# The sums of squares of three norms, moved from GpSimd's queue into VectorE's

## What is computed

```python
def rmsnorm(x, g):
    return x * lax.rsqrt(jnp.mean(x * x, axis=-1, keepdims=True) + EPS) * g

# layer 0: x += concat(short gated convolution, windowed attention)(rmsnorm(x)) @ w_out
# layer 1: x += pool_mix(rmsnorm(x)): window means of 2, 4, 8, 16 tokens minus x, a map per group, a scale
# after each: x += square(relu(rmsnorm(x) @ w_up)) @ w_down      (1024 -> 4096 -> 1024)
```

## Time and profile before

| | us |
|---|---|
| median of three executions | 1857.74 (1857.17 to 1860.59) |
| the profiled execution | 1856.85 |
| its span | 1855.1 |
| TensorE busy (matmul) | 1794.6 |
| VectorE busy | 1286.3 |
| ScalarE busy | 698.8 |
| GpSimd busy | 97.2 |
| the mean granted clock of TensorE | 0.988 of full speed |

### The profile page before, as it was taken

The page is one execution under the profiler, slowest core; times in us unless marked ns, Lnnn a source line. Parts: engine busy times, 40 slices in busy tenths (PEclk is TensorE's granted clock), DMA queues, the critical chain, the costliest instruction groups (busy, mean ns, idle before and its releaser), DMA issues.

```text
span 1855.1 us, 33339 instructions
## 1 busy us (share of the span) xinstructions
PE 1794.6 (97%) x13805; PEld 1752.4 (94%) x13805; DVE 1286.3 (69%) x1992; ACT 698.8 (38%) x1169; POOL 97.2 (5%) x127
## 2 busy tenths in 40 slices
PE   6999999997999999999999999799999999999999
PEld 5998888997999999999999999699999999999999
DVE  4447775469766666878586766787667677868684
ACT  5433332135333333524243355443333353424331
POOL 1100000140000000000000122100000000000000
PEclk9999999999999999999999999799999999999999
DMA  5311111320443444744445212034434484534432
GB/s 196 107 39 35 35 35 53 97 82 25 166 150 135 154 147 153 272 155 162 149 155 179 80 42 79 20 122 152 167 140 143 156 279 144 186 116 169 158 113 95
DMA packets 154519, 233.75 MB, mean 126 GB/s; under 512 B 6800, under 2 KB 103360, under 8 KB 150624
## 3 DMA queue, kind: packets, MB, share of 16 engines
q1 hardware_dynamic: 150880, 222.31, 34.7%
q0 software_dynamic: 3200, 9.21, 1.7%
q10 hardware_dynamic: 288, 0.09, 0.0%
HBM read 160.40 MB, written 71.47 MB: 125 GB/s over the span
## 4 chain that ended last, share of the span: by engine, by line
PE 79%; DVE 11%; ACT 3%; DMA 3%; issue 2%; SPq 1%; POOL 0%; POOLq 0%; DVEq 0%; ACTq 0%
PE out L783 16%; PE out L785 16%; PE out L784 16%; PE scores L785 4%; PE turned L785 4%; PE scores L784 4%; PE turned L784 4%; PE scores L783 4%; PE turned L783 4%; DVE b_lo L2050 1%; DVE ring L2035 1%; DMA wide<-in_w_down 1%; PE turned L965 1%; DVE b_full L2002 1%; DMA wide<-in_w_up 1%
## 5 line engine op out<-in xcount | busy, mean ns | idle before, releaser
L783 PE MATMUL out<-b_hi,ring 128*128 128x268 f32 (+1 forms) x2048 | 590.2, 288 | 23.5 <-DVE b_lo L2066 7.1
L785 PE MATMUL out<-b_hi,ring 128*128 128x268 f32 (+1 forms) x2048 | 589.7, 288 | 0.0
L784 PE MATMUL out<-b_lo,ring 128*128 128x268 f32 (+1 forms) x2048 | 589.3, 288 | 0.0
L1401 ACT ACTIVATE ring<-wide 128x512 fp32r<-128x512 f32 x384 | 233.1, 627 | 552.3 <-DVE wide L2024 225.9
L783 PEld LDWEIGHTS out<-b_hi,ring 128*128 128x128 f32 x2048 | 390.5, 191 | 26.6 <-DVE ring L2035 13.3
L784 PEld LDWEIGHTS out<-b_lo,ring 128*128 128x128 f32 x2048 | 390.1, 190 | 0.1
L785 PEld LDWEIGHTS out<-b_hi,ring 128*128 128x128 f32 x2048 | 390.2, 191 | 0.0
L2035 DVE TENSOR_TENSOR ring<-wide,ring 128x512 fp32r<-128x512 f32 x384 | 261.8, 690 | 154.2 <-ACT ring L1401 152.9
L783 PE MATMUL out<-act_hi,w_hi 128*128 128x352 f32 (+2 forms) x656 | 219.4, 334 | 10.5 <-DVE act_lo L1750 9.2
L783 PE MATMUL turned<-b_hi,ring 128*128 128x268 f32 (+1 forms) x768 | 219.3, 286 | 3.2 <-ACT rs L1385 3.2
L783 PE MATMUL scores<-b_hi,ring 128*128 128x268 f32 (+1 forms) x768 | 219.1, 285 | 2.0 <-DVE ring L2035 2.0
(11 more groups left out here) (204 smaller groups left out, 2593.9 us busy)
## 6 DMA issues: line engine op xcount, KB each, us to landing
wide<-in_w_up SPq DMA_DIRECT2D x32, 1024.0 KB, 5.8
wide<-in_w_down SPq DMA_DIRECT2D x32, 1024.0 KB, 5.6
b_full<-h_dram SPq DMA_DIRECT2D x28, 1072.0 KB, 5.1
b_full<-h_dram SPq DMA_DIRECT2D x28, 1056.0 KB, 5.4
h_dram<-hid SPq DMA_DIRECT2D x64, 268.0 KB, 2.1
h_dram<-hid SPq DMA_DIRECT2D x64, 264.0 KB, 2.2
h_dram<-hid SPq DMA_DIRECT2D x16, 804.0 KB, 3.7
h_dram<-hid SPq DMA_DIRECT2D x16, 792.0 KB, 3.5
```

Of the source, the lines that this page charges most:

```text
L783: nc.tensor.matmul(out, lhs[0], rhs[0], start=first, stop=False, skip_group_check=skip)
L784: nc.tensor.matmul(out, lhs[0], rhs[1], start=False, stop=False, skip_group_check=skip)
L785: return nc.tensor.matmul(out, lhs[1], rhs[0], start=False, stop=last, skip_group_check=skip)
L1401: nc.scalar.activation(cells(ring, n, 0), left_source(U, q), ACT.Copy).then_inc(left_hi, 1)
```

## The change

GpSimd's adds are taken out, with all their waits; nothing but DMA stands in its queue. VectorE gets the same 66 adds, each as its own instruction on the same columns, with the same waits. ScalarE's and TensorE's queues are the same as before, in order and in their waits. Line numbers of the changed kernel are lower by up to 28 ahead of the new functions, and higher by up to 12 behind them.

```diff
-            def add_square(k, c0, c1, begin):
-                pool.wait_ge(sum_begun, begin + 1)
-                pool.wait_ge(squared, k + 1)
-                if k:
-                    pool.wait_ge(added, added_at(k) - 1)
-                n = 1 if k < 28 else 2 if k < 42 else 3
-                nc.gpsimd.tensor_tensor(rs[:, c0:c1], rs[:, c0:c1], square_view(n, k, c1 - c0), ALU.add).then_inc(added, 1)
...
+            def add_square(k, n, p):
+                c0, c1 = NORM_PIECES[n][p] if n != 2 else (HALF_COLS * p, HALF_COLS * (p + 1))
+                dve.wait_ge(sum_begun, begun_no(n, p) + 1)
+                dve.wait_ge(squared, k + 1)
+                if k:
+                    dve.wait_ge(added, added_at(k) - 1)
+                nc.vector.tensor_tensor(rs[:, c0:c1], rs[:, c0:c1], square_view(n, k, c1 - c0), ALU.add).then_inc(added, 1)
...
+                    if a == UNITS - 4 and t in (5, 11, 12, 13):
+                        add_pair_square(a, {5: 1, 11: 3, 12: 4, 13: 5}[t])
+                    if a == UNITS - 2 and t == 1:
+                        add_pair_square(a - 2, 6)
+                        add_pair_square(a - 2, 7)
+                    if a == UNITS - 2 and t in (4, 5, 10, 11, 12, 13):
+                        add_pair_square(a, {4: 0, 5: 1, 10: 2, 11: 3, 12: 4, 13: 5}[t])
...
                     add_output(p, oc)
+                    if p and oc == 0:
+                        add_squares(1, p - 1, 6, 7)
+                    if oc >= 2 and (p < 3 or oc < 7):
+                        add_squares(1, p, oc - 2, oc - 1)
...
+            add_pair_square(UNITS - 2, 6)
+            add_pair_square(UNITS - 2, 7)
             for i in range(10):
...
+                if i == 7:
+                    add_squares(3, 1, 3, 7)
                 add_windows(i)
+                if i in (3, 6, 8):
+                    add_squares(3, {3: 0, 6: 1, 8: 2}[i], 0, 3)
+                if i == 4:
+                    add_squares(3, 0, 3, 7)
...
                 if i == 6:
                     normed(3, 0, 1)
+                if i == 7:
                     left_lo_part(UNITS, A12)
                     first_right_lo(B11, UNITS, 0)
-                if i == 7:
                     first_right_lo(B21, UNITS, 0)
...
+            add_squares(3, 2, 3, 7)
             first_right_lo(B21, UNITS, 1)
+            add_squares(3, 3, 0, 5)
             first_pair(UNITS)
```

More of the change, by code:

```diff
@@ L1980, in _, with add_squares, add_pair_square @@
                         split_lo(W_OUT + 4 + oc // 2)
+            def add_square(k, n, p):
[5 more added lines that the diff above has]
+                nc.vector.tensor_tensor(rs[:, c0:c1], rs[:, c0:c1], square_view(n, k, c1 - c0), ALU.add).then_inc(added, 1)
+            def add_squares(n, p, first, end):
+                for i in range(first, end):
+                    add_square(add_no(n, p) + i, n, p)
+            def add_pair_square(a, t):
+                l, k = pair_square_no(a, t)
+                if k is not None:
+                    add_square(k, 2, l)
             def add_output(p, oc):
```

## The result

The changed kernel took **1878.21 us** (median of 4 runs, 1877.06 to 1882.65). The kernel before took 1858.7 us (median of 4 runs, 1857.17 to 1860.59; one run more than ahead of the prediction). The ratio is 1.0107, with a 95% interval of 1.0094 to 1.0119: slower by 19.9 us, where 17.6 were forecast (1875.3 us). The profiled execution took 1879.21 us; its span of 1877.4 us is 22.3 us longer than that of before.

What follows compares the result with a forecast made beforehand. TensorE (97% busy) was taken to bound the kernel, VectorE from 1142 to 1167 us. Waits 10.8 plus clock 6.8 gave 17.6 us; 1856.85 became 1874.5, with 0.9 for the median 1875.3; range 1872 to 1878.5 (8 in 10: 1865 to 1881).

Steps and rivals of the forecast that it cites:

- More is lost: Rival, 12%: row sums' dip (+1.7), first norm's +1.5, and adds in a row waiting for squares; 1878 to 1882 us.
- this ring: Pooling: VectorE's late add holds ScalarE's square, then the z scaling, then TensorE; +2.9, +3.1, +1.7, +4.0 us at four places.
- Map 5 and map 6: Pooling: TensorE starts these maps late, waiting for z scalings behind squares that need VectorE's adds; +2.9 and +3.1 us.
- Row sums: End of first MLP: the last add TensorE needs stands behind VectorE's last product addition; +1.6 us.
- The size of an add: Price of one add on VectorE by width: 0.44 us at 268 columns, 0.47 at 312, 0.37 at 216.
- First norm: Norm ahead of the first MLP: 26 adds cost 0, bounds -1 to +1.5 us.
- Tail: From tile 9's additions to ScalarE's eight scalings: 5.3 us instead of 7.8, so -2.5 us.
- 4 x 1.7 = 6.8 us: Clock: each of four new TensorE stalls followed by a low clock losing 1.7 us; 6.8 us, bounds 0 to 8.5.
- Waits: New waits at row sums and pooling, less the tail's gain: 1.6 + 2.9 + 3.1 + 1.7 + 4.0 - 2.5 = 10.8 us.
- engine time alone: Rival, 5%: ScalarE is let go in time; only VectorE's added work, row sums and tail count; +3.1 us, 1860.8.
- The waits come, the clock stays: Rival, 25%: the new waits cost 10.8 us but no low clock follows the stalls; 1868.5 us.

Runs made afterwards that it cites:

- Experiments 4 and 6: Against the changed kernel: 4 put second-MLP-norm adds ahead of VectorE's window additions, 1864.31 us; 6 moved ScalarE's scalings of maps 4, 5 ahead of blocked squares, 1870.16 us.
- n1_only: Kernel before with only the 26 adds of the first MLP's norm moved to VectorE, the other 40 left on GpSimd; 1856.03 us (one run).
- warm2: Changed kernel plus 27 unread TensorE matmuls in the four stalls, the last nine ahead of the wait for the windows' input; 1871.5 us, ratio 1.0055.
- tail_only: Kernel before with only the last nine adds of the second MLP's norm moved to VectorE; 1858.9 us, ratio 0.9994.
- early: Changed kernel with the second MLP's norm adds placed earlier in VectorE's queue, ahead of the window additions; 1864.31 us, ratio 1.0023.
- early_warm: early_rowsum plus eight unread TensorE matmuls: six ahead of the mean product behind map 8, two ahead of tile 9's windows; 1861.73 us, ratio 1.0003.
- before_warm: Kernel before plus eight unread TensorE matmuls: six ahead of the mean product behind map 8, two ahead of tile 9's windows; 1861.18 us, ratio 1.0003.
- n2_only: Kernel before with only the 14 adds of the pooling's norm moved to VectorE, all others left on GpSimd; 1864.64 us (one run).
- act_order: Changed kernel with, on ScalarE alone, the scalings of maps 4 and 5 moved ahead of the blocked squares; 1870.16 us (one run).
- warm: Changed kernel plus 27 unread TensorE matmuls for the four stalls, the last nine behind the wait for z; 1876.3 us, ratio 1.009.
- n3_only: Only the second MLP's norm's 26 adds on VectorE, steps placed as in the changed kernel, other norms on GpSimd; 1879.35 us, ratio 1.0098.
- early_rowsum: early with the last pooling-norm add that the row sums wait for one product addition earlier on VectorE; 1861.17 us, ratio 1.0006.

## Why the prediction was right, and where it was off

The direction, the place and the kind of the loss were forecast. The time came out 2.9 us above the forecast of 1875.3 and 0.3 us inside its range, and part of that is luck: the profiled spans grew by 22.3 us where 17.6 were forecast, while the median lies 1.0 us below the profiled execution where 0.9 above was assumed. The measured 1878.21 also lies in the range of the second rival, "More is lost" (1878 to 1882), so the number alone doesn't decide between them; the terms do.

- **Direction and mechanism: right.** Four stalls, at maps 5, 6, 8 and windows 9, with the scaling of z as releaser, each behind a square that waits for an add. Experiments 4 and 6 break this ring from either side: VectorE's order, and all four stalls go; ScalarE's at maps 5 and 6, and those two go.
- **Map 5 and map 6 (2.9 and 3.1):** 2.85 and 3.15. **Row sums (1.6):** 1.72, of which 1.48 is the stall itself. The size of an add was right to 0.02 us.
- **First norm (0, with -1 to +1.5):** -1.03, at the edge of its bounds. The prediction let VectorE's four waits for ScalarE in this stretch take in 0.9 us of the adds. They were 1.14, 1.14, 1.14 and 1.40 us before and are 0.79, 0.19, 0.79 and 0.94 now, so they took in 2.1; with the prediction's other terms, 5.0 - 3.9 - 2.1 = -1.0. n1_only, with this norm's adds alone, has the same four waits (0.79, 0.21, 0.79, 0.94); that they and nothing else make the difference is a sum and not an experiment. The profiled run hid it, since its clock fell once more in the set-up, at 310 to 316 us (0.72 over that stretch, 1.00 before), which is 1.7 us.
- **Tile 6:** not in the forecast. Its window additions shift back by 1.39 us. The eight multiplications of 47 columns took 2.89 us beside GpSimd's adds and 1.51 without. I had counted that gift for the 216-column ones alone.
- **Tail (-2.5):** -1.93. The nine adds took 4.8 us (2.33 + 2.44) in place of 3.9, since some wait for their squares. VectorE's wait of 10.02 us is now 3.90, as forecast.
- **Clock, the step that was mis-sized: "I take 4 x 1.7 = 6.8 us", and no dip behind the row sums.** Measured: 1.6 behind the row sums, 1.55, 2.33, 1.1 at map 8 (from its start to the window additions of tile 7 it is 1170.85 - 1165.16 = 5.69 us, where the forecast took 4.55), and 4.8 in the windows of tile 9 (10.4 us in place of 5.6), together 11.4, outside the stated bounds of 0 and 8.5. The four that I had counted came to 9.8. The premise was that every fall lasts as long as the one in the earlier trace rows. At the last stall it lasted 16.8 us. warm2 gives 9.2 for B, in agreement.
- **Waits:** the five of B without the clock were forecast as 2.9 + 3.1 + 1.7 + 4.0 - 2.5 = 9.2; measured 8.5 by the steps of the table (18.3 less 9.8), 9.1 by warm2. The 8.5 has tile 6's -1.4 in it, which was not forecast; without it the waits came to some 9.8, 0.6 over their forecast.

Of the rivals, engine time alone is refuted by experiment 4: the adds stay on VectorE and 15.6 of 19.9 us vanish. "The waits come, the clock stays" is what warm2 made by hand, 1871.5 us, 10.8 above the kernel before that ran beside it, which is that rival's 10.8 (its 1868.5). "More is lost" was half right: the row sums' dip came (+1.6), the first norm's loss did not, and the largest part of what was lost more, 3.1 us in the windows of tile 9 (4.8 in place of 1.7), it did not name. The sentence of the Trainium skill (Perfetto Trace Analysis, "Optimizing Scalar/DVE Operations"), that moving work between VectorE and GpSimd might not help since they share a port, points to something these traces show: GpSimd's adds slowed VectorE's short instructions by up to 1.9 us in a group, and taking them away paid for much of the adds' own time. Read as engine time it gave 1860.8 us, and the changed kernel missed that by 17 us.

Left open: the lasting low clock in the windows of tile 9. It came in the changed kernel with a stall of 4.77 us, but in tail_only behind one of 1.32 and in early behind one of 0.45. Nor is it shown that the stall alone brings it. The kernel before fell too, at 1166.9, when these windows were just done; early, early_warm and before_warm, which start them 2.6 to 3.3 us later, fell at 1167 to 1168, with the windows still running; warm2, its stall filled, fell in their last 2 us. So the work of this stage may bring a fall of its own, which then lies in the windows when they start late. Filling the stall took the windows from 10.4 to 6.5 us; how much of the rest is whose, and what decides between a short and a long fall, I can't say from these runs.

## What to carry to other kernels

When an operation moves to another engine, ask first where it lands in that queue and who waits for its semaphore: an add of 0.48 us cost 3 us a time because ScalarE's next scaling stood behind a square that waited for it, and the same adds placed one step earlier cost almost nothing. Price each TensorE stall on the critical chain twice, once for its length and once for the clock behind it, and give the second a wide bound: here it was forecast at 6.8 us and came to 11.4. Where the effect looked for is 2 us and runs scatter by 5, compare the wait or the stretch itself across traces; the median can't settle it.

## What the runs showed that I had not expected

- **The clock falls where nothing was edited.** The profiled run of the changed kernel has 0.72 over 310 to 316 us, that of the kernel before 1.00; at 450 to 456 us it is the other way round (1.00 and 0.72). The fall at 310 us costs 1.7, since TensorE is busy there throughout (6.00 us of 6.00). Such falls come at a few places, in one trace and not in the other: near 310 us in nine of the thirteen, near 324 in seven, near 1571 in four, and at none of the three in that of the kernel before. The kernel before ran between 1857.05 and 1864.03 us in these studies; such falls are a likely cause, not a shown one, as only one of its runs has a trace.
- **A stall does not always bring a fall.** The same 1.48 us ahead of the row sums was followed by one in three traces (changed, n2_only, act_order: A is 1.6 longer) and not in three others (early, warm, warm2).
- **Filling a stall kept the clock.** With 5, 6 and 7 unread matmuls in the first three stalls the granted clock stayed at 1.00 in both traces, where the changed kernel fell to about 0.5 three times.
- **GpSimd's adds slow short VectorE instructions.** Eight multiplications of 47 columns took 2.88 or 2.89 us in each of four traces with GpSimd adding at that time (before, n1_only, n2_only, tail_only), and 1.51 in four without (changed, n3_only, early, early_rowsum). Four of 216 columns took 3.42 us before and 1.50 in the changed kernel.
